# Values of two head pairs made together every second step, with a third pair of turned buffers

## The chip, the cores and the metric

The kernel runs on one core of a Trainium2 chip. The metric is the device time of one execution in microseconds (us). Five engines work side by side, each through its own queue in order: PE multiplies matrices and writes only to the eight banks of PSUM, DVE and ACT compute and copy, POOL does small work and starts some transfers, SP starts transfers. They wait for one another through semaphores. In the profile PE is the row of products and PEld the row of weight loads that go with them.

## The reference

The reference is one step of a small transformer with two layers on 640 tokens (512 latent, 128 context), model width 1024, all in 32-bit floats. In each layer three attentions run side by side, their outputs are joined and projected, and a mixture of 16 experts follows. What is changed here is the latent attention: 8 heads, whose queries and keys have 96 columns and whose values have 64.

```python
k, v = mla_expand(ckv, kpe, w_ukv_l)           # per head: 96 key columns, 64 value columns
s = einsum('bqkgd,bskd->bkgqs', q_blk, k) * scale
p = softmax(s, axis=-1)
o = einsum('bkgqs,bskv->bqkgv', p, v)
x = x + g1 * einsum('bte,ed->btd', heads_out, w_out_l)
```

A latent token reads the 512 latent keys and the 128 context keys, so five blocks of 128; a context token reads the 128 context keys only, one block.

## The kernel before

Each layer runs in stages: modulation and input projection, windowed and neighbourhood attention ("phase 2" in the code), the expansion of queries, keys and values of the latent attention, the latent attention itself ("phase 4"), and the experts. The change touches phase 4, which also holds the output projection, the second norm and the routing.

Phase 4 works on 20 pairs of heads, `pairs[p]`: five tiles of 128 tokens in the order context tile, then four latent tiles, and four pairs of heads for each. Pairs 0 to 3 (context) have one block of keys, `n` = 1; pairs 4 to 19 have `n` = 5. The work is written out by hand in numbered steps `s`, from 0 to 29, the same on every engine. In step `s`, for head `h` = 0 and then 1, PE makes the scores of pair `s` (`scores`, line 588, into banks 0 and 1 or 2 and 3) and turns the normalised probabilities of pair `s-3` (`turn`, transposes, line 520, into banks 4 and 5). Then it makes the values of pair `s-4` (`values`, line 614) into bank 6: one product for each block of keys and head, and the two heads stand in different halves of the 128 columns of the array and of the 128 partitions of the bank. Then comes what the code calls `beside`: for tile `i`, with `PROJ[i]` = 4`i`+8,

- steps `PROJ`+0 and `PROJ`+1: the two halves of the output projection (`out`, line 741, 8 products into bank 7);
- steps `PROJ`+2 and `PROJ`+3: the two halves of the updated tile are transposed (`h2`, line 520, 4 products into bank 7);
- a step with routing logits (line 679) and one with ranks (lines 668 and 669), both into bank 6.

The last tile (`i` = 4) has a table of its own after step 24.

DVE makes in step `s` the row maxima of pair `s` (line 1837), copies the last two turned blocks of pair `s-3` out of bank 5 (line 1871), then evicts what lies in bank 7 in `projected`: line 1926 multiplies a half of the output projection by its gate and line 1927 hands the bank back; line 1930 does this for the second half of `h2`. Only after that it normalises pair `s-1` (lines 1881 and 1884). ACT copies the first three turned blocks (line 1257), takes the exponentials (line 1248), copies the finished values out of bank 6 (`outputs`, line 1262) and evicts the first half of `h2` (line 1305).

The order is held by counters, the lanes: `S` for the score banks, `T` for banks 4 and 5, `O` for bank 6, `M` for bank 7. `take` makes PE wait until everything handed out before on that lane was given back. So each job in bank 7 waits for DVE or ACT to have emptied the job before it. The turned blocks lie in `pt[4]`, two pairs of buffers used in turn; the copy of pair `p` waits for the values of pair `p-2`.

Of the kernel before, what the change touches and what calls it, by code (L numbers as in the profile page):

```python
# [29 lines left out]
ACT = mybir.ActivationFunctionType  # L30
AX = mybir.AxisListType

P = 128
# [39 lines left out]
AT = [ORDER.index(t) for t in range(TILES)]  # L73
# [67 lines left out]
def program(nc, t_in, t_out):  # L141
    with ExitStack() as ctx:
# [18 lines left out]
        hoT = big[:, 1024:6144].rearrange("p (t k n) -> p t k n", t=TILES, k=KD)  # L161
        mrow = sb("mrow", [P, 3, 512])
# [41 lines left out]
        cqT, o = place(0, 2, TOK)  # L204
        ckvT, o = place(o, KEYS)
# [6 lines left out]
        v_loc, o = place(A0, KVT, 384)  # L212
        qs, o = place(o, 2, TOK)
        qn, o = place(o, 2, TOK)
        ksT, o = place(o, KEYS)
        knT, A1 = place(o, 2, KEYS)

        rowG2, o = place(A1, 2, D)
        proj, o = place(o, 2, PW)
        rt, o = place(o, 2, 384)  # L220
        ck, o = place(o, 544)
        junk1, o = place(o, 192)
        assert o <= 4 * 4096
        y1, o = place(4 * 4096, 2, D)
        y2, o = place(o, 2, D)
# [18 lines left out]
        rq, o = place(o, 2, 256)  # L244
        pb4 = ring[:, 0:5120].rearrange("p (a b n) -> p a b n", a=DEEP, b=2)
        pt4a, o = place(A3, 4, 640)
        pt4 = [[pt4a[:, 0], pt4a[:, 1]], [pt4a[:, 2], pt4a[:, 3]]]
        h2T, o = place(o, D)
        junk4, o = place(o, 256)
        r_T, o = place(o, NE)  # L250
# [234 lines left out]
        def value_rows(pr, h, j):  # L485
            if pr["kind"] == "mla":
                return v_mla[:, j, pr["heads"][h] * 64:pr["heads"][h] * 64 + 64]
            at = 64 * h if pr["kind"] == "swa" else 128 + 64 * pr["heads"][h]
            return v_loc[:, j, at:at + 64]

        def column(p, h):
            return slice(2 * (p % 4) + h, 2 * (p % 4) + h + 1)

# [14 lines left out]
        def turned(phase, p, h, w):  # L508

            if phase == 2 and p < WIDE:  # L510
                return ps[:, 4 + h, 0:w]
            return two(2, w) if phase == 2 and p >= APART and h else two(4, w)
# [5 lines left out]
        def _(pe):  # L518
# [52 lines left out]
            def attention(L, phase):  # L571
# [34 lines left out]
                    mm.then_inc(T.full, 1)  # L606

                def values(p):
                    pr = pairs[p]
                    O.take(pe, ("o", L, phase, p))  # L610
                    pe.wait_ge(T.free, T.freed[("p", L, phase, p, 1)])
                    for j in range(pr["n"]):
                        for h in range(2):
                            mm = pe.matmul(ps[64 * h:64 * h + 64, 6, 0:P], value_rows(pr, h, pr["v"][j]),  # L614
                                           pt[phase][p % 2][h][:, j * P:(j + 1) * P],
                                           start=(j == 0), stop=(j == pr["n"] - 1))
                    mm.then_inc(O.full, 1)

                for s in range(STEPS[phase]):
                    turning = 3 <= s < len(pairs) + 3  # L620
                    if phase == 4:
                        ranks(L, s - 1)
                    if phase == 2:
                        together = turning and (s - 3 < WIDE or s - 3 > APART)
                        if turning:
                            turn(s - 3, 0)
                        if together:
                            turn(s - 3, 1)
                        if s < len(pairs):
                            scores(s, (0, 1))  # L630
                        if s in (1, 2):
                            spin(7, 3 - s)
                        if turning and not together:
                            turn(s - 3, 1)
                        if s == len(pairs) + 1:
                            pe.wait_ge(nmax_done, base + 2 * len(pairs))
                        if s > len(pairs):
                            spin(3, 1)
                    else:
                        for h in range(2):  # L640
                            if s < len(pairs):
                                scores(s, (h,))
                                if s == 0:
                                    spin(7, 2)
                            if turning:
                                turn(s - 3, h)
                    if 4 <= s < len(pairs) + 4:
                        values(s - 4)
                    if phase == 2:
                        for g, at in enumerate(MOD_AT):  # L650
                            if s in (at, at + 1) and (g < 2 or L < DEPTH - 1):
                                ks = range(4 * (s - at), 4 * (s - at) + 4)
                                mod_group(L + g // 2, (g + 1) % 3, ks)
                        for g in (1, 2):
                            if s == MOD_AT[g - 1] + 3:
                                mod_columns2(L, g)
                        if s == MOD_AT[2] + 3 and L < DEPTH - 1:
                            mod_columns(L + 1)
                    if phase == 4:
                        if s == 1:  # L660
                            shift_logits(L)
                        beside(L, s)
# [566 lines left out]
        def _(act):  # L1229
            def attention(L, phase):  # L1230
                pairs = PAIRS[phase]
                base = PPL * L + PBASE[phase]

                def exps(p, h):

                    pr, w, col = pairs[p], pairs[p]["n"] * P, column(p, h)
                    buf = pb[phase][:, p % DEEP, h, :]
                    act.wait_ge(nmax_done, base + 2 * p + h + 1)
                    if pr["kind"] == "swa":
                        act.wait_ge(sink_set, SINKS * L + sum(2 * (r["kind"] == "swa") for r in pairs[:p]) + h + 1)  # L1240
                    if phase == 4 and p >= DEEP:
                        act.wait_ge(T.full, T[("p", L, phase, p - DEEP, h)])
                    if phase == 2:
                        w += int(pr["kind"] == "swa")
                        act.activation(buf[:, 0:w], buf[:, 0:w], ACT.Exp, bias=stat["nm"][:, col], scale=-1.0,  # L1245
                                       accum_out=stat["sm"][:, col]).then_inc(ex_done, 1)
                    else:
                        act.activation(buf[:, 0:w], two(2 * h, w), ACT.Exp, bias=stat["nm"][:, col], scale=1.0,  # L1248
                                       accum_out=stat["sm"][:, col]).then_inc(S[h].free, 1)

                def copy(p, h):
                    n = pairs[p]["n"]
                    a, d = split(phase, n)
                    act.wait_ge(T.full, T[("p", L, phase, p, h)])
                    if p >= 2:
                        act.wait_ge(O.full, O[("o", L, phase, p - 2)])
                    act.activation(pt[phase][p % 2][h][:, 0:a * P], turned(phase, p, h, a * P), ACT.Copy).then_inc(T.free, 1)  # L1257

                def outputs(p):
                    pr = pairs[p]  # L1260
                    act.wait_ge(O.full, O[("o", L, phase, p)])
                    act.activation(hoT[:, AT[pr["t"]], pr["chunk"], :], ps[:, 6, 0:P], ACT.Copy).then_inc(O.free, 1)

                for s in range(STEPS[phase]):
                    turning = 3 <= s < len(pairs) + 3
                    if phase == 2:
                        for h in range(2):
                            if turning:
                                copy(s - 3, h)
                        for h in range(2):  # L1270
                            if s < len(pairs):
                                exps(s, h)
                    else:
                        for h in range(2):
                            if turning:
                                copy(s - 3, h)
                            if s < len(pairs):
                                exps(s, h)
                    if 4 <= s < len(pairs) + 4:
                        outputs(s - 4)  # L1280
                    if phase == 4:
                        beside(L, s)
# [406 lines left out]
        def _(dve):  # L1689
# [140 lines left out]
            def attention(L, phase):  # L1830
# [34 lines left out]
                def copy(p, h):  # L1865
                    a, d = split(phase, pairs[p]["n"])
                    if d:
                        dve.wait_ge(T.full, T[("p", L, phase, p, h)])
                        if p >= 2:
                            dve.wait_ge(O.full, O[("o", L, phase, p - 2)])  # L1870
                        dve.tensor_copy(pt[phase][p % 2][h][:, a * P:(a + d) * P], ps[:, 5, 0:d * P]).then_inc(T.free, 1)  # L1871

                def normalise(p):
                    w = pairs[p]["n"] * P
# [533 lines left out]
```

## Time and profile before

| | |
|---|---|
| time, median of 3 runs | 1313.77 us (1312.25 to 1314.42) |
| the profiled execution's own time | 1311.26 us |
| its span, first to last instruction | 1309.3 us |
| PE busy | 1263.0 us, 96% |
| DVE, ACT, POOL busy | 604.7, 354.4, 152.5 us |
| mean granted TensorE clock | 0.992 |
| phase 4 in layer 0 and in layer 1 | about 277 to 441 us and 905 to 1067 us |

PE is busy for 96% of the span, and a product counts as busy until its end, so neighbouring products overlap in the rows: the pace of PE is read from the starts, not from the lengths. A row of the timeline merges instructions of one line that follow each other; its length reaches to the end of the last.

### The profile page before, as it was taken

Reading aid. Unit: us, or ns where it says so; the run is one execution under the profiler, and the core shown is the slowest. Engines: PE = TensorE matmul, PEld = TensorE weight load, DVE = VectorE, ACT = ScalarE, POOL = GpSimd, SP = SyncE. Lnnn points to the kernel's source line nnn. Section 1 sums busy time; section 2 is a strip of 40 time slices with the busy share of each in tenths; the row PEclk is TensorE's granted clock in tenths of the full one; section 3 lists DMA queues with packets and bytes.
Section 4 is the critical chain, followed back from the end, with each engine's and each line's share of the span. In section 5 each row is a group of like instructions: output and inputs, shape, how many; then the busy total and the mean of one; then the engine's idle time right before and its main releaser. Section 6 shows DMA issues by size and latency. Waiting matters only on the chain. (4 is left out here: it accounts for less than half of the span.)

```text
span 1309.3 us, 17044 instructions
## 1 busy us (share of the span) xinstructions
PE 1263.0 (96%) x6010; PEld 724.4 (55%) x6010; DVE 604.7 (46%) x1519; ACT 354.4 (27%) x933; POOL 152.5 (12%) x257
## 2 busy tenths in 40 slices
PE   6999999999999999999999999999999999999997
PEld 3555555565665565444455556566566556444442
DVE  0132266345665553433344235654556646344438
ACT  1121266334433111000012115663433321000001
POOL 2201130000000120000142003000000012000014
PEclk9999999989999999999999999999999999999999
DMA  9977997699011699999694039423001159999966
GB/s 356 364 245 244 316 371 265 227 353 305 25 65 65 242 343 378 366 370 368 242 349 156 17 123 351 151 99 105 1 33 65 65 195 350 391 365 374 367 257 244
DMA packets 125439, 313.13 MB, mean 239 GB/s; under 512 B 9882, under 2 KB 58426, under 8 KB 112688
## 3 DMA queue, kind: packets, MB, share of 16 engines
q1 hardware_dynamic: 90896, 243.13, 51.0%
q0 software_dynamic: 12848, 45.39, 9.1%
q10 hardware_dynamic: 21616, 23.60, 5.4%
q8 instruction: 45, 0.74, 0.2%
q14 instruction: 34, 0.28, 0.1%
HBM read 232.14 MB, written 80.71 MB: 239 GB/s over the span
## 5 line engine op out<-in xcount | busy, mean ns | idle before, releaser
L820 PE MATMUL ps<-ring,big 128*128 128x384 f32 (+2 forms) x640 | 230.6, 519 | 1.5 <-DVE big L1804 1.3
L820 PEld LDWEIGHTS ps<-ring,big 128*128 128x128 f32 x640 | 120.3, 190 | 104.2 <-issue 63.7
L901 PE MATMUL ps<-ring,arena 128*128 128x512 f32 x384 | 169.3, 593 | 1.9 <-ACT arena L1437 1.9
L741 PE MATMUL ps<-ring,big 128*128 128x512 f32 x320 | 143.0, 599 | 0.9
L520 PEld LDWEIGHTS ps<-consts,arena 128*128 128x128 f32 (+2 forms) x880 | 103.6, 143 | 69.1 <-issue 50.9
L588 PE MATMUL ps<-arena 64*128 64x128 f32 (+5 forms) x576 | 136.2, 428 | 2.4 <-ACT ring L1248 1.4
L520 PE MATMUL ps<-consts,arena 128*128 128x128 f32 (+2 forms) x880 | 123.4, 277 | 4.7 <-ACT arena L1390 2.5
L1257 ACT ACTIVATE arena<-ps 128x384 f32<-128x384 f32 (+3 forms) x140 | 67.3, 492 | 199.3 <-PE ps L520 198.5
L901 PEld LDWEIGHTS ps<-ring,arena 128*128 128x128 f32 x384 | 71.2, 190 | 83.1 <-issue 83.1
L588 PEld LDWEIGHTS ps<-arena 64*128 64x128 f32 (+1 forms) x576 | 74.4, 194 | 53.4 <-issue 45.1
L741 PEld LDWEIGHTS ps<-ring,big 128*128 128x128 f32 x320 | 59.0, 190 | 70.5 <-issue 66.4
L1441 ACT ACTIVATE arena<-ps 128x256 f32<-128x256 f32 x32 | 12.3, 385 | 300.6 <-PE ps L901 300.6
L1837 DVE TENSOR_REDUCE st_nm<-ps 128x1 f32<-128x640 f32 (+1 forms) x80 | 57.2, 717 | 74.6 <-PE ps L588 74.2
L614 PE MATMUL ps<-arena 128*64 128x128 f32 x1104 | 85.9, 280 | 1.4 <-DVEq L2005 1.4
L2164 DVE TENSOR_TENSOR arena<-arena,ps 128x256 f32<-128x256 f32 x32 | 13.5, 421 | 154.4 <-ACT arena L1441 154.4
L614 PEld LDWEIGHTS ps<-arena 128*64 128x64 f32 x1104 | 66.5, 137 | 13.1 <-issue 8.4
L2182 DVE TENSOR_TENSOR arena<-ps,arena 128x512 f32<-128x512 f32 x64 | 44.2, 691 | 55.1 <-PE ps L922 55.1
L1248 ACT ACTIVATE ring<-ps,st_nm 128x640 f32<-128x640 f32 (+1 forms) x80 | 56.4, 705 | 19.7 <-DVE st_nm L1837 19.3
L922 PE MATMUL ps<-ring,arena 128*128 128x512 f32 x128 | 57.8, 594 | 1.0 <-DVE arena L2170 1.0
L922 PE MATMUL ps<-arena 128*128 128x512 f32 x128 | 57.8, 594 | 1.0 <-DVE arena L2170 1.0
L1245 ACT ACTIVATE arena<-arena,st_nm 128x640 f32<-128x640 f32 (+4 forms) x80 | 53.6, 673 | 17.3 <-DVE st_nm L1862 16.0
L520 PE MATMUL ps<-consts,ring 128*128 128x128 f32 x336 | 51.9, 278 | 5.3 <-ACT arena L1257 4.4
(238 smaller groups left out, 1467.6 us busy)
## 6 DMA issues: line engine op xcount, KB each, us to landing
ring<-in_w_mod SPq DMA_DIRECT2D x40, 1024.0 KB, 12.1
ring<-in_w_up SPq DMA_DIRECT2D x22, 1024.0 KB, 9.4
ring<-in_w_gate SPq DMA_DIRECT2D x22, 1024.0 KB, 6.8
slots<-zeros ACTq DMA_DIRECT2D x8, 2560.0 KB, 14.7
slots<-zeros SPq DMA_DIRECT2D x8, 2560.0 KB, 20.4
arena<-in_w_down SPq DMA_DIRECT2D x16, 1024.0 KB, 12.3
arena<-slots SPq DMA_DIRECT2D x30, 512.0 KB, 5.5
slots<-arena POOLq DMA_DIRECT2D x30, 512.0 KB, 9.3
```

The costliest lines, as they stand in the source:

```text
L520: return pe.transpose(out, in_, ident)
L588: mm = pe.matmul(two(score_bank(phase, p, h))[:, at:at + hi - lo], queries(pr, h), keys(pr, h, lo, hi), start=(at % 512 == 0), stop=True, ...
L614: mm = pe.matmul(ps[64 * h:64 * h + 64, 6, 0:P], value_rows(pr, h, pr["v"][j]), pt[phase][p % 2][h][:, j * P:(j + 1) * P], start=(j == 0), ...
L741: mm = pe.matmul(ps[:, b, :], hoT[:, i, k, :], slot[2 + half][:, k, :], start=(k == 0), stop=(k == KD - 1))
L820: mm = pe.matmul(ps[:, c, 0:CHUNKS[c][1]], hT[:, s, k, :], slot[c][:, k, 0:CHUNKS[c][1]], start=(k == 0), stop=(k == KD - 1))
L901: mm = pe.matmul(ps[:, b, :], xgT[:, b, k * P:(k + 1) * P], w_gu[q][:, :, k, :], start=(k == 0), stop=(k == KD - 1))
L922: mm = pe.matmul(ps[:, 2 + n, :], hidT[:, b, k * P:(k + 1) * P], w_dn[q][:, k, n * 512:(n + 1) * 512], start=(k == 0), stop=(k == 1))
L1245: act.activation(buf[:, 0:w], buf[:, 0:w], ACT.Exp, bias=stat["nm"][:, col], scale=-1.0, accum_out=stat["sm"][:, col]).then_inc(ex_done, 1)
L1248: act.activation(buf[:, 0:w], two(2 * h, w), ACT.Exp, bias=stat["nm"][:, col], scale=1.0, accum_out=stat["sm"][:, col]).then_inc(S[h].free, 1)
L1257: act.activation(pt[phase][p % 2][h][:, 0:a * P], turned(phase, p, h, a * P), ACT.Copy).then_inc(T.free, 1)
L1837: dve.tensor_reduce(nm, two(2 * h, w), AX.X, ALU.max, negate=True).then_inc(nmax_done, 1)
L2182: return TT(yb[:, b, n * 512:(n + 1) * 512], ps[:, 2 + n, :], rowG[:, n * 512:(n + 1) * 512], ALU.mult)
```

## The change

The values of phase 4 are made in every second step. In odd steps `s` (5 to 23) PE makes the values of pairs `s-5` and `s-4` one behind the other, side by side in bank 6 (columns 0 to 127 and 128 to 255), and ACT copies both out with one instruction of 256 columns. In even steps no values are made and none copied out. Phase 2 stays as it is. Since a pair's turned blocks are now kept one step longer, `pt[4]` has a third pair of buffers, which lies in `mrow`, the rows in which the modulation vectors are made; a wait for `mods_out` (the transfer of these rows to memory, awaited by SP ahead of phase 4 already) stands before its first use.

```diff
-        pt4 = [[pt4a[:, 0], pt4a[:, 1]], [pt4a[:, 2], pt4a[:, 3]]]
+        mflat = mrow.rearrange("p a b -> p (a b)")
+        pt4 = [[pt4a[:, 0], pt4a[:, 1]], [pt4a[:, 2], pt4a[:, 3]], [mflat[:, 0:640], mflat[:, 640:1280]]]
...
+        def turned_rows(phase, p, h):
+            return pt[phase][p % len(pt[phase])][h]
+        def value_group(phase, p):
+            if phase == 2:
+                return (p,)
+            return (p - 1, p) if p % 2 else ()
+        def values_before(phase, p):
+            q = p - len(pt[phase])
+            return q if q < 0 or phase == 2 or q % 2 else q + 1
...
                 def values(p):
-                    pr = pairs[p]
+                    group = value_group(phase, p)
                     O.take(pe, ("o", L, phase, p))
                     pe.wait_ge(T.free, T.freed[("p", L, phase, p, 1)])
-                    for j in range(pr["n"]):
-                        for h in range(2):
-                            mm = pe.matmul(ps[64 * h:64 * h + 64, 6, 0:P], value_rows(pr, h, pr["v"][j]),
-                                           pt[phase][p % 2][h][:, j * P:(j + 1) * P],
+                    for g, q in enumerate(group):
+                        pr = pairs[q]
+                        for j in range(pr["n"]):
+                            for h in range(2):
+                                mm = pe.matmul(ps[64 * h:64 * h + 64, 6, g * P:(g + 1) * P], value_rows(pr, h, pr["v"][j]),
+                                               turned_rows(phase, q, h)[:, j * P:(j + 1) * P],
...
-                    if 4 <= s < len(pairs) + 4:
+                    if 4 <= s < len(pairs) + 4 and value_group(phase, s - 4):
                         values(s - 4)
...
-                    if p >= 2:
-                        act.wait_ge(O.full, O[("o", L, phase, p - 2)])
+                    q = values_before(phase, p)
+                    if q >= 0:
+                        act.wait_ge(O.full, O[("o", L, phase, q)])
+                    if phase == 4 and p == 2:
+                        act.wait_ge(mods_out, 32 * (L + 1))
...
-                    act.activation(hoT[:, AT[pr["t"]], pr["chunk"], :], ps[:, 6, 0:P], ACT.Copy).then_inc(O.free, 1)
+                    n = len(value_group(phase, p))
+                    act.activation(hoT[:, AT[pr["t"]], pr["chunk"] + 1 - n:pr["chunk"] + 1, :],
+                                   ps[:, 6, 0:n * P].rearrange("p (a b) -> p a b", a=n), ACT.Copy).then_inc(O.free, 1)
```

DVE's copy waits in the same way as ACT's, with the wait for `mods_out` at its own first use of the third pair (`p` = 5).

On PE, the end of step 9 and step 10 of layer 0 stand so before (line 588 scores, 520 transposes, 614 values, 741 output projection; `ps` is PSUM, `ring` holds the probabilities and the weights of the projection, `big` the tile that `h2` transposes):

```order
L614 MATMUL ps<-arena 64x128 [waits t_free,o_free]
L614 MATMUL ps<-arena 64x128 x9
L741 MATMUL ps<-ring,big 128x512 [waits o_free,slot3_in,m_free]
L741 MATMUL ps<-ring,big 128x512 x7
...
L588 MATMUL ps<-arena 128x512 [waits s1_free]
L588 MATMUL ps<-arena 128x128
L520 MATMUL ps<-consts,ring 128x128 [waits pn_done,t_free]
L520 MATMUL ps<-consts,ring 128x128 x4
L614 MATMUL ps<-arena 64x128 [waits t_free,o_free]
L614 MATMUL ps<-arena 64x128 x9
L520 MATMUL ps<-consts,big 128x128 [waits res_done,m_free]
L520 MATMUL ps<-consts,big 128x128 x3
```

and so after the change (the lines are those of the changed file: 604 scores, 536 transposes, 632 values, 759 output projection):

```order
L632 MATMUL ps<-arena 64x128 [waits t_free,o_free]
L632 MATMUL ps<-arena 64x128 x9
L632 MATMUL ps<-mrow,arena 64x128 x10
L759 MATMUL ps<-ring,big 128x512 [waits o_free,slot3_in,m_free]
L759 MATMUL ps<-ring,big 128x512 x7
...
L604 MATMUL ps<-arena 128x512 [waits s1_free]
L604 MATMUL ps<-arena 128x128
L536 MATMUL ps<-consts,ring 128x128 [waits pn_done,t_free]
L536 MATMUL ps<-consts,ring 128x128 x4
L536 MATMUL ps<-consts,big 128x128 [waits res_done,m_free]
L536 MATMUL ps<-consts,big 128x128 x3
```

The ten values of step 10 have moved ahead into those of step 11, and the transposes of `h2`, which wait for bank 7 (`m_free`), stand directly behind those of the probabilities.

On ACT, steps 9 and 10 had two copies out of bank 6 (line 1262; 1257 are the copies of turned blocks, 1248 the exponentials):

```order
L1262 ACTIVATE big<-ps 128x128 [waits o_full]
L1257 ACTIVATE arena<-ps 128x384 [waits o_full,t_full]
L1248 ACTIVATE ring,st_sm<-ps,st_nm 128x640 [waits t_full,nmax_done]
L1257 ACTIVATE arena<-ps 128x384 [waits o_full,t_full]
L1248 ACTIVATE ring,st_sm<-ps,st_nm 128x640 [waits t_full,nmax_done]
L1262 ACTIVATE big<-ps 128x128 [waits o_full]
L1292 ACTIVATE arena,ssq<-big 128x512 [waits res_done]
```

and have one of double width at the end of step 9 (the lines of the changed file: 1284, 1278, 1266, 1315):

```order
L1284 ACTIVATE big<-ps 128x256 [waits o_full]
L1278 ACTIVATE arena<-ps 128x384 [waits o_full,t_full]
L1266 ACTIVATE ring,st_sm<-ps,st_nm 128x640 [waits t_full,nmax_done]
L1278 ACTIVATE arena<-ps 128x384 [waits o_full,t_full]
L1266 ACTIVATE ring,st_sm<-ps,st_nm 128x640 [waits t_full,nmax_done]
L1315 ACTIVATE arena,ssq<-big 128x512 [waits res_done]
```

The copy at the end of step 10 is gone; nothing else on ACT has changed its place. DVE's order is the same in both kernels, except that some of its copies go to `mrow`.

## Rows read from the trace of the kernel before

**Rows 1.** The page, busy time of each engine, its share and instructions.
```profile
PE 1263.0 (96%) x6010; PEld 724.4 (55%) x6010; DVE 604.7 (46%) x1519; ACT 354.4 (27%) x933; POOL 152.5 (12%) x257
```
**Rows 2.** Stretches: length, busy time (instructions) of each engine, clock, DMA share, GB/s.
```profile
277.00:441.30 164.30, 158.68 (x924) 101.17 (x922) 91.95 (x230) 62.21 (x173) 8.55 (x15) 0.98 0.41 135
441.30:790.00 348.70, 343.34 (x1120) 183.21 (x1119) 136.01 (x294) 44.40 (x119) 47.36 (x75) 1.00 0.75 279
905.00:1067.00 162.00, 156.99 (x908) 99.17 (x906) 90.90 (x227) 60.84 (x170) 8.53 (x15) 0.97 0.18 61
```
**Rows 3.** PE's timeline, steps 7 to 10: start, length, instructions [idle before].
```profile
304.05 0.44 PE L614 MATMUL ps<-arena 128*64 128x128 f32 x4
304.42 1.35 PE L588 MATMUL ps<-arena 96*128 96x512 f32 x4
305.61 0.71 PE L520 MATMUL ps<-consts,ring 128*128 128x128 f32 x5
306.15 1.25 PE L588 MATMUL ps<-arena 96*128 96x512 f32 x4
307.23 0.71 PE L520 MATMUL ps<-consts,ring 128*128 128x128 f32 x5
307.88 1.31 PE L614 MATMUL ps<-arena 128*64 128x128 f32 x20
309.12 7.13 PE L741 MATMUL ps<-ring,big 128*128 128x512 f32 x16
...
319.44 1.31 PE L614 MATMUL ps<-arena 128*64 128x128 f32 x20
320.87 7.13 PE L741 MATMUL ps<-ring,big 128*128 128x512 f32 x16
...
330.55 0.71 PE L520 MATMUL ps<-consts,ring 128*128 128x128 f32 x5
331.19 1.31 PE L614 MATMUL ps<-arena 128*64 128x128 f32 x20
332.61 0.66 PE L520 MATMUL ps<-consts,big 128*128 128x128 f32 x4
```
**Rows 4.** DVE's timeline, end of step 10.
```profile
331.49 0.41 DVE L1871 COPY arena<-ps 128x256 f32<-128x256 f32 x1
331.82 0.68 DVE L1926 TENSOR_TENSOR big<-ps,arena 128x512 f32<-128x512 f32 x1
```
**Rows 5.** Who waited for whom on PEld: us in total, times, longest.
```profile
PEld ps L588 <- ACT ring L1248: 3.2, 8, 0.9
PEld ps L520 <- DVEq L1927: 2.5, 8, 0.4
PEld ps L741 <- DVEq L1927: 2.5, 8, 0.4
PEld ps L741 <- DVE arena L1930: 1.5, 6, 0.3
```
**Rows 6.** PE's timeline, step 20 and the values of step 23.
```profile
413.57 1.31 PE L614 MATMUL ps<-arena 128*64 128x128 f32 x20
414.82 7.13 PE L741 MATMUL ps<-ring,big 128*128 128x512 f32 x16
...
438.63 1.31 PE L614 MATMUL ps<-arena 128*64 128x128 f32 x20 [0.62 <-DVEq L2005]
```
**Rows 7.** DVE's timeline, end of step 20.
```profile
414.02 0.68 DVE L1930 TENSOR_TENSOR arena<-ps,modc 128x512 f32<-128x512 f32 x1
```
**Rows 8.** Stretches as in rows 2, around low clock and in step 22.
```profile
283.67:287.09 3.42, 2.78 (x25) 2.58 (x24) 0.96 (x5) 0.46 (x3) 0.00 (x0) 1.00 1.04 348
287.09:293.92 6.83, 6.78 (x18) 3.98 (x19) 2.42 (x9) 2.76 (x11) 0.00 (x0) 0.50 1.03 343
911.70:922.00 10.30, 10.17 (x24) 5.23 (x23) 4.01 (x11) 4.62 (x15) 0.00 (x0) 0.50 0.33 123
433.70:438.60 4.90, 3.73 (x39) 3.00 (x37) 2.57 (x9) 2.48 (x8) 0.00 (x0) 1.00 0.04 13
```

More of the change, by code:

```diff
@@ L608, in values @@
                 def values(p):
-                    pr = pairs[p]
+                    group = value_group(phase, p)
                     O.take(pe, ("o", L, phase, p))
                     pe.wait_ge(T.free, T.freed[("p", L, phase, p, 1)])
-                    for j in range(pr["n"]):
-                        for h in range(2):
-                            mm = pe.matmul(ps[64 * h:64 * h + 64, 6, 0:P], value_rows(pr, h, pr["v"][j]),
-                                           pt[phase][p % 2][h][:, j * P:(j + 1) * P],
-                                           start=(j == 0), stop=(j == pr["n"] - 1))
+                    for g, q in enumerate(group):
[4 more added lines that the diff above has]
+                                               turned_rows(phase, q, h)[:, j * P:(j + 1) * P],
+                                               start=(j == 0), stop=(j == pr["n"] - 1))
                     mm.then_inc(O.full, 1)
@@ L1254, in copy @@
                     act.wait_ge(T.full, T[("p", L, phase, p, h)])
-                    if p >= 2:
-                        act.wait_ge(O.full, O[("o", L, phase, p - 2)])
-                    act.activation(pt[phase][p % 2][h][:, 0:a * P], turned(phase, p, h, a * P), ACT.Copy).then_inc(T.free, 1)
+                    q = values_before(phase, p)
[3 more added lines that the diff above has]
+                        act.wait_ge(mods_out, 32 * (L + 1))
+                    act.activation(turned_rows(phase, p, h)[:, 0:a * P], turned(phase, p, h, a * P), ACT.Copy).then_inc(T.free, 1)
                 def outputs(p):
@@ L1278, in attention @@
                                 exps(s, h)
-                    if 4 <= s < len(pairs) + 4:
+                    if 4 <= s < len(pairs) + 4 and value_group(phase, s - 4):
                         outputs(s - 4)
@@ L1868, in copy @@
                         dve.wait_ge(T.full, T[("p", L, phase, p, h)])
-                        if p >= 2:
-                            dve.wait_ge(O.full, O[("o", L, phase, p - 2)])
-                        dve.tensor_copy(pt[phase][p % 2][h][:, a * P:(a + d) * P], ps[:, 5, 0:d * P]).then_inc(T.free, 1)
+                        q = values_before(phase, p)
+                        if q >= 0:
+                            dve.wait_ge(O.full, O[("o", L, phase, q)])
+                        if p == 5:
+                            dve.wait_ge(mods_out, 32 * (L + 1))
+                        dve.tensor_copy(turned_rows(phase, p, h)[:, a * P:(a + d) * P], ps[:, 5, 0:d * P]).then_inc(T.free, 1)
                 def normalise(p):
```

## The prediction, written before the changed kernel ran

> **What bounds the kernel now.** I read the page first, then the stretches, then the timelines around the values. PE is busy for 1263.0 us of 1309.3 [rows 1]. In phase 4 it is busy for 158.68 of 164.30 us in layer 0 and 156.99 of 162.00 in layer 1, and in the experts of layer 0 for 343.34 of 348.70 [rows 2]; DVE and ACT have much time left everywhere. So PE's own sequence sets the time: what is added to it or taken from it reaches the end of the kernel almost whole, because the experts behind it have no wait that could swallow it. The question is how long PE takes from the start of step 4 to the end of step 23.
>
> **What a group of values costs.** PE's pace is read from starts [rows 3]. Five transposes followed by scores take 306.15 - 305.61 = 0.54 us; followed by values they take 307.88 - 307.23 = 0.65, so entering the group costs 0.11. The twenty rows of one pair (each 32-bit product is two) take until 309.12, so 1.24. Without the group the projection could start at 307.23 + 0.54 = 307.77; the group costs 309.12 - 307.77 = 1.35 there. Behind it the first product is slow as well: four scores take 1.35 us behind values and 1.25 behind transposes, 0.10 more. One group standing alone costs 1.45 us. The pace inside: four rows last 0.44, twenty 1.31, so 0.87/16 = 0.054 each, and twenty more rows appended to a group cost 20 x 0.054 = 1.09. A merge that is bare of waits therefore saves 1.45 - 1.09 = 0.36 us. There are 10 merges per layer, 20 in all: up to 7.2 us. That is the whole possible gain on PE.
>
> The Trainium skill, "TensorEngine Tiling (Array Packing)", section "Key Properties", gives a reason for such a saving: a change of the tiling mode drains the engine. The rows agree that both edges of the group cost something (0.11 and 0.10 us); by that rule alone the change would bring the 7.2 us, to about 1306.6.
>
> **What the group hides.** Behind the values of most steps stands a job for bank 7, and it waits until DVE has emptied that bank. DVE reaches this eviction only after its copy of the last turned blocks, that is, after the transposes directly ahead of the values. Step 10 shows it: the transposes start at 330.55 and end 0.71 later at 331.26 [rows 3]; DVE copies from 331.49, multiplies out of bank 7 from 331.82 to 332.50 [rows 4]; PE goes on at 332.61 [rows 3]. PE could have gone on at 330.55 + 0.54 = 331.09. All 1.52 us between are DVE's chain, and the values lie inside it. Take them away and PE starts the next job at 332.61 all the same: this step saves nothing. The waits that stick out behind the values today mark the places [rows 5]: 8 times the transposes of `h2` behind line 1927 (steps 10, 14, 18, 22 of two layers), 6 times the projection behind line 1930 (steps 12, 16, 20), and 8 times the projection behind line 1927 (odd steps 9, 13, 17, 21).
>
> **The sum, over two layers.**
> - Odd steps 9 to 23, eight per layer: each gets ten more products behind those it has, 16 x 1.09 = +17.4 us. In step 23 the values wait for the ranks first (0.62, line 2005 [rows 6]); this wait is ahead of the group and hides nothing of the addition.
> - Step 8: nothing is in bank 7 to wait for, since the projection of tile 0 is the first job there since step 1, and in the rows it starts without an idle time [rows 3]. Its group goes whole: 2 x -1.45 = -2.9.
> - Even steps 10, 12, 14, 16, 18, 22: 0 each, hidden in DVE's chain. If the cover were only partly needed, each would save up to 1.45 (12 x 1.45 = 17.4 at the other end). I take 0, because rows 3 and 4 show the chain to run past the group already and its start, the end of the transposes, does not move.
> - Step 20: DVE is done at 414.02 + 0.68 = 414.70 [rows 7], PE went on at 414.82 [rows 6]: at most 0.1 each, I take 2 x -0.05 = -0.1.
> - Odd steps 9, 13, 17 had a wait left behind the values: 320.87 - 319.44 = 1.43 instead of 1.24 [rows 3], 0.19. A double group covers it: 6 x -0.18 = -1.1. Step 21 shows none.
> - Steps 4 to 7, pairs with one block (four rows, 0.44 long [rows 3]): the scores there wait for exponentials anyway (3.2 us in 8 waits [rows 5]), so a removed group of four rows saves little, and four rows more in steps 5 and 7 cost 4 x 0.054 = 0.2 each, partly in those waits. I take +0.1 per layer, +0.2. The ends: four small groups removed whole, each up to about 0.5, would be -2.0; nothing hidden, +0.9.
> - ACT's copy of 256 columns in place of two of 128, and the new wait for `mods_out`: 0. ACT is busy for 62 of 164 us of the phase [rows 2], its one copy per two steps stands ahead of nothing that PE awaits before the next turned blocks, and the transfer had ended before phase 4 began (SP waited for it). Were the wait real, ACT's copies and exponentials from step 5 on would queue behind it.
> - The wait of the turned-block copies for earlier values: always values of a step before; those precede the transposes on PE. 0.
>
> Sum: 17.4 - 2.9 - 0.1 - 1.1 + 0.2 = +13.5 us. Against the profiled execution's own 1311.26 this is 1324.8; that execution lies 2.5 under the median of the runs shown, so for the median 1313.77 + 13.5 = 1327.3.
>
> **Rival 1: the clock falls as well.** The granted clock was at its lower level (1.2 instead of 2.4 GHz) from 287.09 to 293.92 and for about 10.3 us from 911.7 [rows 8]; ahead of the first, PE was busy for only 2.78 of 3.42 us, much of it with products of 24 columns. At the end of phase 4 there are already stretches in which PE does little but transposes, rank products and waits: 433.7 to 438.6 has 3.73 us busy in 4.90 [rows 8], and 1.2 of these are the values of step 22, which now go. Step 20 is of the same kind (a wait for ACT between its transposes, then, without values, one of 1.1 us). So up to two places per layer could bring the lower level. Each such stretch, 6.8 to 10.3 us long, costs half its length, 3.4 to 5.1 us, since dense projection products follow. With one or two of them in the whole kernel 1331 to 1337, with four up to 1347. Against it: the stretches did not drop the clock before, and the gaps of 1.5 us in steps 10 to 18 stand between dense work. The Trainium skill, "TensorE: Matmul & The Clock Gate", Part 4 on the PE-mode transpose, says that transposes do not count as busy in the way that products do; that would speak for this rival, and no row here shows it by itself.
>
> **Rival 2: the gain comes through (the other side).** If DVE emptied bank 7 earlier than its place in the order suggests, the even steps would be bare and all 20 merges would save 0.36: -7.2, 1306.6. It decides at the chain's length: DVE would have to be done within 0.54 us of the start of the transposes, not 1.95 (330.55 to 332.50) as in rows 3 and 4. Nothing in the change moves DVE's instructions, so this speaks against it.
>
> **Rival 3: half of it.** Some even steps save part of their group, because later starts give DVE time to catch up elsewhere, or because a wait in the odd steps (turned blocks in steps 11 and 15) shrinks. At half of the added cost in the even steps, 6 x 0.6 x 2 = 7 us less: 1320. At equal chance of no net effect, 1313.8, it would take 1.1 us from each of the twelve even steps, which none of the chain's rows supports.
>
> **How the numbers follow.** Forecast (stalls, clock as before) 0.52; clock falls too 0.32; half of it 0.08; no net effect 0.04; the gain 0.04. The forecast's own range is 1324 to 1330, from the ends of steps 4 to 7 and run-to-run noise. The range of 8 in 10 takes in most of rival 1 and the upper part of rival 3: 1319 to 1338. What a measurement of this kernel can tell is about 0.2% or 2.6 us. Faster 0.04, same 0.04, slower 0.92.
>
> **What would show it.** The values group appears as 40 rows, about 2.4 us long, eight times per layer, with no idle before the job behind it in odd steps. In the even steps 10 to 22 PE's row has a new idle time of 1.2 to 1.6 us ahead of `h2` or the projection, put down to DVE, about 14 in two layers and some 19 us in total; PE's busy time stays nearly the same while the span grows. In step 8 the projection starts 0.54 us after the transposes. A third and fourth low stretch in the clock near the end of phase 4 would be rival 1. The prediction is wrong if the idle times in the even steps are well under 1 us, or if the odd steps' additional products take less than 1.09 us.

## The result, and the profile after

The changed kernel takes 1329.24 us (median of 4 runs, 1325.61 to 1332.50) against 1314.10 for the kernel before (1312.25 to 1315.38): a ratio of 1.0116, with its 95% interval 1.0093 to 1.0138. Its profiled execution took 1327.09 us, its span is 1325.1. The comparison of the totals comes first. The second row is the busy time of each engine in the page of the changed kernel:

```profile
span 1325.1 us, 17004 instructions
PE 1261.8 (95%) x6010; PEld 726.3 (55%) x6010; DVE 604.9 (46%) x1519; ACT 351.7 (27%) x913; POOL 152.4 (12%) x257
```

Against [rows 1] PE has as many instructions and is busy for 1.2 us less, with a span 15.8 us longer. The loss is idle time on PE, and the waits name it. PE's waits in the trace of the changed kernel (us in total, times, longest):

```profile
PE ps L536 <- DVEq L1953: 10.5, 8, 1.4
PE ps L759 <- DVE arena L1956: 7.4, 6, 1.3
PE ps L604 <- ACT ring L1266: 3.4, 6, 0.7
PE ps L536 <- ACT arena L1278: 2.3, 4, 0.6
PE ps L536 <- ACT mrow L1278: 1.2, 2, 0.6
```

Two rows of the same view of the kernel before, for ACT's copies of turned blocks and for the exponentials:

```profile
PE ps L520 <- ACT arena L1257: 4.4, 6, 1.1
PE ps L588 <- ACT ring L1248: 1.4, 2, 0.7
```

The first two rows of the changed kernel are new: 14 waits, 17.9 us in all, for DVE's products out of bank 7. The numbers of lines have moved: 536 is 520 of before (transposes), 604 is 588 (scores), 632 is 614 (values), 759 is 741 (projection), 1953 and 1956 are 1927 and 1930, 1897 is 1871 (DVE's copy of turned blocks), 1860 is 1837 (maxima). The first 8 and the next 6 are exactly the even steps 10 to 22 of both layers. PEld's rows, which answer to [rows 5], say the same; the 8 waits of the projection for line 1927, in the odd steps, have gone:

```profile
PEld ps L536 <- DVEq L1953: 12.4, 8, 1.6
PEld ps L759 <- DVE arena L1956: 8.8, 6, 1.5
PEld ps L604 <- ACT ring L1266: 5.1, 8, 0.9
```

PE's timeline of the changed kernel, the end of steps 8, 9 and 10 (start, length, instructions, [idle before]), answers to [rows 3]:

```profile
308.98 0.71 PE L536 MATMUL ps<-consts,ring 128*128 128x128 f32 x5
309.53 0.59 PE L759 MATMUL ps<-ring,big 128*128 128x512 f32 x1
...
319.11 0.71 PE L536 MATMUL ps<-consts,ring 128*128 128x128 f32 x5
319.75 1.31 PE L632 MATMUL ps<-arena 128*64 128x128 f32 x20
320.89 1.26 PE L632 MATMUL ps<-mrow,arena 128*64 128x128 f32 x20
322.08 0.70 PE L759 MATMUL ps<-ring,big 128*128 128x512 f32 x1
...
331.76 0.71 PE L536 MATMUL ps<-consts,ring 128*128 128x128 f32 x5
333.83 0.55 PE L536 MATMUL ps<-consts,big 128*128 128x128 f32 x3 [1.35 <-DVEq L1953]
```

In step 8 the projection follows the transposes at once. In step 9 both pairs run together: 322.08 - 319.75 = 2.33 us, against 1.43 before. In step 10 PE stands still for 1.35 us. From the start of the transposes to the next job it takes 333.83 - 331.76 = 2.07 us; before, with the values in between, it took 332.61 - 330.55 = 2.06 [rows 3]. So the step costs the same with its values and without. DVE at that place in the changed kernel:

```profile
331.96 0.82 DVE L1860 TENSOR_REDUCE st_nm<-ps 128x1 f32<-128x640 f32 x1 [0.48 <-PE ps L604]
332.70 0.41 DVE L1897 COPY arena<-ps 128x256 f32<-128x256 f32 x1
333.03 0.68 DVE L1952 TENSOR_TENSOR big<-ps,arena 128x512 f32<-128x512 f32 x1
```

It is the chain of [rows 4]: maxima, copy of the turned blocks, product out of bank 7 until 333.71, and PE goes on 0.12 us later.

Two stretches show the whole phase, from the start of step 8 to the first product of `out(4,0)`; first the kernel before, then the changed one (length, busy time and instructions of each engine, clock, DMA share, GB/s):

```profile
304.42:441.32 136.90, 132.88 (x797) 83.56 (x795) 77.73 (x193) 48.62 (x130) 8.57 (x15) 1.00 0.28 94
```

```profile
306.17:450.81 144.64, 132.89 (x796) 84.67 (x795) 77.64 (x192) 47.21 (x122) 9.65 (x16) 0.99 0.27 90
...
370.40:373.70 3.30, 1.95 (x13) 1.35 (x12) 3.05 (x7) 2.81 (x9) 0.00 (x0) 1.00 0.02 5
373.70:377.10 3.40, 3.40 (x10) 2.17 (x9) 2.00 (x9) 1.48 (x4) 1.24 (x2) 0.50 0.69 217
1052.90:1056.30 3.40, 3.40 (x6) 1.33 (x4) 1.68 (x3) 0.00 (x0) 0.00 (x0) 0.50 0.00 0
```

PE is busy for the same 132.9 us and the stretch is 7.74 us longer. 1.7 of these are not idle time: from 373.70 to 377.10 the clock stands at its lower level (1.2 GHz; the column says 0.50 of 2.4). Just ahead of it PE was busy for 1.95 us of 3.30, with the new idle time of step 14 in between. Layer 1 has a stretch like it from 1052.90, behind step 20. At neither place had the trace of the kernel before a low stretch. A part of every comparison here is time lost at the lower clock, and it differs from run to run of one kernel. So beside each median stands a second number. The time lost at the low clock is estimated as (1 - mean granted clock) x span of the same run, as if PE set the pace all through the low stretches; the time less this loss is called the corrected time below. The clock of a run is on record to three digits, so one run's corrected time is known to about 0.7 us. For 29 runs of the kernel before beside the first four experiments it is 1299.5 us at the median (1297.4 to 1301.6), where the times themselves go from 1309.8 to 1321.1; for the four runs of the changed kernel it is 1313.1 (1311.4 to 1313.8). These two sets did not run side by side; a second pair that did gives 1300.5 and 1313.8 (after_again, below). The change costs 13.6 us in corrected time, and the time lost at the low clock grew from 14.4 to 16.6 us at the medians.

### The profile page after: what moved, and what is told of

The parts are those of the page before. It is cut to its first block and busy times, and to the rows that moved or that the text cites. A ratio compares the mean times of both kernels' runs of the same rounds, so it can differ in the third digit from the quotient of the medians.

```text
span 1325.1 us, 17004 instructions
## 1 busy us (share of the span) xinstructions
PE 1261.8 (95%) x6010; PEld 726.3 (55%) x6010; DVE 604.9 (46%) x1519; ACT 351.7 (27%) x913; POOL 152.4 (12%) x257
## 5 line engine op out<-in xcount | busy, mean ns | idle before, releaser
L604 PE MATMUL ps<-arena 64*128 64x128 f32 (+5 forms) x576 | 135.6, 427 | 4.3 <-ACT ring L1266 3.4
L604 PEld LDWEIGHTS ps<-arena 64*128 64x128 f32 (+1 forms) x576 | 74.6, 195 | 54.4 <-issue 44.5
L1278 ACT ACTIVATE arena<-ps 128x384 f32<-128x384 f32 (+3 forms) x116 | 56.4, 499 | 158.2 <-PE ps L536 158.0
L2190 DVE TENSOR_TENSOR arena<-arena,ps 128x256 f32<-128x256 f32 x32 | 13.5, 421 | 154.4 <-ACT arena L1464 154.4
L632 PE MATMUL ps<-arena 128*64 128x128 f32 x896 | 69.6, 278 | 1.4 <-DVEq L2031 1.4
L1266 ACT ACTIVATE ring<-ps,st_nm 128x640 f32<-128x640 f32 (+1 forms) x80 | 56.4, 705 | 19.3 <-DVE st_nm L1860 19.0
L632 PEld LDWEIGHTS ps<-arena 128*64 128x64 f32 x896 | 55.7, 136 | 8.4 <-issue 3.7
## 6 DMA issues: line engine op xcount, KB each, us to landing
ring<-in_w_mod SPq DMA_DIRECT2D x40, 1024.0 KB, 11.9
arena<-in_w_down SPq DMA_DIRECT2D x16, 1024.0 KB, 11.8
```

Of the source, the lines that this page charges most:

```text
L604: mm = pe.matmul(two(score_bank(phase, p, h))[:, at:at + hi - lo], queries(pr, h), keys(pr, h, lo, hi), start=(at % 512 == 0), stop=True, ...
L632: mm = pe.matmul(ps[64 * h:64 * h + 64, 6, g * P:(g + 1) * P], value_rows(pr, h, pr["v"][j]), turned_rows(phase, q, h)[:, j * P:(j + 1) * ...
L1278: act.activation(turned_rows(phase, p, h)[:, 0:a * P], turned(phase, p, h, a * P), ACT.Copy).then_inc(T.free, 1)
```

## The experiments

Theory: DVE's place for the eviction of bank 7 makes the even steps as long without their values as with them. Rivals: the removed values would have been free anyway; the new buffers and their waits cost something; the clock costs it.

**DVE empties bank 7 first, in the changed kernel (after_evict_first).** The call of `projected` goes ahead of the maxima and the copies, except for the first projection:

```diff
+                        if s - 1 != PROJ[0]:
+                            projected(L, s - 1)
...
-                    if phase == 4 and s >= 1:
+                    if phase == 4 and s - 1 == PROJ[0]:
```

> The changed kernel with one thing moved: in each step of phase 4 (but the one of the first projection half) DVE empties bank 7 at the start of its step, ahead of its row maxima and copies, and not behind the copy of the last turned blocks. Theory (the loss is DVE's chain behind the transposes, which the values covered): the 14 idle times of 1.1 to 1.5 us in the even steps vanish, about 18 to 20 us; all merges then pay 0.36 us each. Against before: minus 7 for the merges, minus 1 to 2.5 for the waits that before has behind its values, so 1304 to 1308 us where before has 1314. Rival (the clock's additional low stretches are a main part of the loss): the time stays 3 to 5 us above that. Rival (DVE's own work is too long for an early place, since it then delays the maxima by 0.7 us in every step): part of the idle time comes back ahead of scores or transposes, 1310 to 1320 us.

Measured: 1310.21 us (12 runs, 1308.07 to 1312.86), a ratio of 0.9971 (0.9955 to 0.9987) to the kernel before; corrected 1297.2, so 15.9 less than the change. PE's timeline, steps 10 and 11, and the waits of this kernel:

```profile
332.19 0.71 PE L536 MATMUL ps<-consts,ring 128*128 128x128 f32 x5
332.74 0.60 PE L536 MATMUL ps<-consts,big 128*128 128x128 f32 x4
333.18 1.25 PE L604 MATMUL ps<-arena 96*128 96x512 f32 x4
334.26 0.71 PE L536 MATMUL ps<-consts,ring 128*128 128x128 f32 x5
334.81 1.25 PE L604 MATMUL ps<-arena 96*128 96x512 f32 x4
337.12 0.76 PE L536 MATMUL ps<-consts,ring 128*128 128x128 f32 x5 [1.06 <-DVE mrow L1897]
337.81 2.40 PE L632 MATMUL ps<-arena 128*64 128x128 f32 x40
```

```profile
PE ps L536 <- DVE arena L1897: 6.9, 8, 1.2
PE ps L536 <- DVE mrow L1897: 2.1, 2, 1.1
```

All 14 waits for bank 7 are gone: behind the transposes of step 10 the next job starts after 0.55 us. That shows where the idle time came from: DVE's order, and not the work of the even steps. The intervals of the 14 steps shrink by 20.2 us (from 1.63, 1.57, 1.39 and 1.45 to 0.11 between the starts of the last transpose and of the next job), yet only 15.9 arrive, and the time is above the 1304 to 1308 us that were expected. Ten waits for DVE's copies of turned blocks, 9.0 us, stand where the changed kernel has two such waits, 0.8 us, and 2.3 us more for ACT's copies. That is 5.9 us more of waits for copies, enough for the missing 4.3, though these waits were not taken away by themselves. In step 11 the copy stands behind maxima which could start only when an earlier product of DVE was done, and PE's transposes wait for the copy. This is DVE's timeline there:

```profile
335.31 0.69 DVE L2054 TENSOR_TENSOR big<-big,arena 128x512 f32<-128x512 f32 x1
335.92 0.82 DVE L1860 TENSOR_REDUCE st_nm<-ps 128x1 f32<-128x640 f32 x1
336.65 0.41 DVE L1897 COPY mrow<-ps 128x256 f32<-128x256 f32 x1
```

**The same order without merged values (before_evict_first).** The same edit in the kernel before.

> The kernel before, with the same move of DVE's eviction of bank 7 to the start of the step and nothing else. Theory: the 22 short waits behind the values go, which stick out by 0.1 to 0.2 us each: minus 1 to 3 us, 1311 to 1313 us, so that the change's two parts interact: merging costs 15 us with the late eviction and gains 5 to 7 with the early one. Rival (the early eviction is a gain by itself of 10 us or more, whatever the values do): 1304 us or less.

Measured: 1314.35 us (12 runs), ratio 1.0006 (0.9989 to 1.0023), where 1311 to 1313 was expected; corrected 1297.1, so 2.4 less than before and level with after_evict_first. The 2.4 us do not show in the time, since 17.1 us are lost at the low clock, against 14.4 in the kernel before: the trace of this kernel has low stretches in phase 4 at 427.4 and 1052.0, where the kernel before has none, and one of 17 us from 287.5, where it has 6.8. In times the merged kernel is 4.1 us ahead, and 4.0 of that is the difference in time lost at the low clock (17.1 against 13.1). In the 12 runs of each the loss is 13.1 to 21.1 us here and 11.8 to 14.4 in after_evict_first, so this is more than scatter; whether the merged values bring it or something else was not tried. The order alone is worth 2.4 us corrected where the values stand in every step, and 15.9 (1313.1 - 1297.2) where they are merged: only there had PE been left with nothing else to do. That merging brings nothing in corrected time under this order was not expected. Here PE waits less for the copies than in after_evict_first:

```profile
PE ps L520 <- DVE arena L1871: 4.6, 4, 1.2
```

That is 4.4 us less than the 9.0 there, and the waits for exponentials are 1.4 us against 2.7. Together 5.7 of the 7.2 us that merging could have saved stand in these waits; that they ate the saving is read from the two traces and was not tested.

**The third buffers without the merging (third_buffers_alone).**

```diff
-            if phase == 2:
-                return (p,)
-            return (p - 1, p) if p % 2 else ()
+            return (p,)
...
-            return q if q < 0 or phase == 2 or q % 2 else q + 1
+            return q
```

> The changed kernel with its values made in every step again, one pair each, and copied out singly; only the third pair of turned buffers in the modulation rows and the waits for them are left of the change. Theory: as before, 1313 to 1315 us, since the copies never waited for the values of an earlier step. Rival (the rows in mrow or their wait for mods_out cost something): over 1317 us, with idle time of ACT ahead of the copy of pair 2.

Measured: 1314.55 us (10 runs), ratio 1.0009 (0.9988 to 1.0030); corrected 1299.1 against 1299.5. The buffers in the modulation rows and the wait for `mods_out` cost nothing that can be measured. One wait is shorter in this trace than before: between the transposes of step 20 PE waits 0.58 us for ACT's copy in each layer, where it waited 1.05 and 1.01. In sum its waits for ACT's copies are 3.5 us in 6 waits, against the 4.4 in 6 above.

**Products on zeros in the idle times (after_spin, and again beside a second run of the change, after_again).** Ahead of bank 7's job of the even steps 10 to 22 PE gets two products on zeros (four rows) into bank 6, once ACT has emptied it, to see whether the clock hangs on the idle time:

```diff
+                    if phase == 4 and s in (10, 12, 14, 16, 18, 20, 22):
+                        pe.wait_ge(O.free, O.frees)
+                        spin(6, 2)
```

> The changed kernel with two filler products of 256 columns of zeros into bank 6 (0.85 us on PE) in steps 10, 12, 14, 16, 18, 20 and 22, where PE otherwise stands idle for 1.1 to 1.5 us. Theory: the fillers lie inside the idle time, which stays put down to DVE, so they cost nothing; and PE is active in it, so the additional low stretches of the clock in phase 4 (one in each layer of the profiled run) go: 1325 to 1328 us and less scatter than the 7 us of the changed kernel. Rival (the low stretches have nothing to do with the idle times): the same low stretches and 1325 to 1333 us. Rival (the eviction is not what PE waits for): the fillers add to the time, up to 12 us.

Measured: 1324.34 us (6 runs, 1323.58 to 1327.64); corrected 1313.2, the same as the change's 1313.1. Repeated together:

> The changed kernel itself, beside the run with fillers on the same chip. Theory: 1326 to 1333 us; with the low clock taken off 1312.5 to 1313.5 us, that is 13 to 14 above before's 1299.5, as forecast; the rest of its loss is time at the low clock, which differs from run to run.

> The changed kernel with the fillers in the even steps, as in after_spin, on the same chip as after_again. Theory (the idle times of the even steps bring some of the low stretches): 2 to 5 us below after_again, and as much in the time at the low clock; with that taken off, equal within 0.5 us. Rival (the difference between the first two sets was chance of the runs): the two within 1 us, also in the time at the low clock.

Measured: after_again 1328.99 us (4 runs, 1326.14 to 1331.44), corrected 1313.8; after_spin_again 1327.36 (5 runs, 1325.35 to 1328.08), corrected 1315.0. Step 10 in the trace of after_spin, and the stretches around the place where the clock of the changed kernel had dropped:

```profile
331.64 0.71 PE L536 MATMUL ps<-consts,ring 128*128 128x128 f32 x5
332.19 1.03 PE L541 MATMUL ps<-zeros 128*128 128x256 f32 x4
333.71 0.66 PE L536 MATMUL ps<-consts,big 128*128 128x128 f32 x4 [0.49 <-DVEq L1956]
```

```profile
370.00:373.40 3.40, 2.91 (x19) 2.22 (x18) 3.11 (x7) 2.85 (x10) 0.00 (x0) 1.00 0.00 0
373.40:380.00 6.60, 6.60 (x64) 4.98 (x63) 4.35 (x14) 4.02 (x11) 2.23 (x3) 1.00 0.76 277
```

The step is as long as in the changed kernel (333.71 - 331.64 = 2.07 us): the added 1.03 us lie wholly inside the idle time. The clock stays at 2.4 GHz there, and neither filled trace has a low stretch in phase 4 from step 8 on; after_again has two, in layer 1 (1045.1 to 1048.5 and 1055.3 to 1058.7), and a third right behind the phase (from 1082.6). The time lost at the low clock falls by 5.4 us in the first pair (16.6 to 11.2) and 4.0 in the second (15.9 to 11.9); in the 8 runs without the products on zeros it is 10.6 to 20.0, in the 11 with them 9.3 to 13.3. The times differ by 4.9 and by 1.6 us; the second is below what was expected, since the corrected time of those runs was 1.2 us higher, about the scatter of this number over a few runs. So products in the idle times take away some of the low clock, worth 2 to 5 us in the two pairs, but not the 13.6 us. They take away more than the change had brought: 11.2 and 11.9 us are less than the 14.4 and 13.1 of the kernel before.

**Merged values with an order made for them (merged_order), and that order alone (single_order).** From the experiments so far: values of the first four pairs single again, DVE empties bank 7 early, in steps 21 and 22 between the copies of the two heads, and in steps 11, 15 and 19 the copy goes ahead of the maxima.

```diff
-            if phase == 2:
+            if phase == 2 or p < 4:
                 return (p,)
...
+                    late, between = s - 1 == PROJ[0], s in (21, 22)
...
+                        if not late and not between:
+                            projected(L, s - 1)
...
+                        copy_first = phase == 4 and h == 0 and s in (11, 15, 19)
+                        if copy_first:
+                            copy(s - 3, h)
...
+                        if phase == 4 and h == 0 and between:
+                            projected(L, s - 1)
```

> The changed kernel (values of two pairs together) with DVE's order in phase 4 fitted to it: bank 7 emptied at the start of the step, in steps 21 and 22 between the copies for the two heads; in steps 11, 15 and 19 the copy of the turned blocks of head 0 ahead of the row maximum, not behind it; and the values of the four short pairs made singly again in steps 4 to 7. Theory: with bank 7 emptied early the merges' 7 us went into new waits of PE for DVE's copies of turned blocks (0.67 us more in each of steps 11, 15 and 19, 0.65 in steps 21 and 22, in both layers); with these copies early, 5 to 8 us come back: 1302 to 1306 us where the kernel before has 1314 and the same kernel with the early eviction alone 1310. With the time lost at the low clock taken off ((1 - mean granted clock) x span), 1289 to 1292 after 1297. Rival (DVE's backlog only moves on to the maxima and so to the scores): 1308 to 1311 us, waits of scores for exponentials in steps 12, 16 and 20.

> The kernel before (values of one pair in each step) with the same order of DVE as the run beside it (bank 7 emptied early, copy of head 0 first in steps 11, 15, 19). Theory: merging is worth 0.36 us for each of 16 merges of full pairs once nothing waits, so this one lies 4 to 6 us above merged_order; it gains 1 to 2 us on the early eviction alone from the copies (waits of 0.57, 0.07 and 0.07 us per layer) and up to 1 us from step 22: 1294 to 1296 us with the low clock taken off. Rival (merging is worth nothing in itself, the edges of the group are hidden in some other limit): the two within 1.5 us of each other.

Measured: merged_order 1306.88 us (6 runs, 1305.28 to 1310.33), ratio 0.9951 (0.9936 to 0.9965), corrected 1293.4; single_order 1311.28 (10 runs, 1306.74 to 1317.31), ratio 0.9985 (0.9967 to 1.0002), corrected 1295.8; the kernel before beside them 1313.41, corrected 1300.5. merged_order stays above what was expected of it (1302 to 1306 us, corrected 1289 to 1292), and single_order lies where it was expected in corrected time. merged_order beats both kernels: it is 0.49% faster than before, against 1.16% slower for the change. Merging in this order is worth 4.4 us in times and 2.4 corrected, more than the rival of no gain allowed (1.5 us). The bare saving of 8 merges per layer, 16 x 0.36 = 5.8 us, does not come whole. Steps 10 and 11 of merged_order:

```profile
334.78 0.71 PE L536 MATMUL ps<-consts,ring 128*128 128x128 f32 x5
335.33 0.60 PE L536 MATMUL ps<-consts,big 128*128 128x128 f32 x4
335.76 1.25 PE L604 MATMUL ps<-arena 96*128 96x512 f32 x4
336.85 0.71 PE L536 MATMUL ps<-consts,ring 128*128 128x128 f32 x5
337.39 1.25 PE L604 MATMUL ps<-arena 96*128 96x512 f32 x4
339.02 0.77 PE L536 MATMUL ps<-consts,ring 128*128 128x128 f32 x5 [0.38 <-ACT mrow L1278]
339.71 2.40 PE L632 MATMUL ps<-arena 128*64 128x128 f32 x40
```

```profile
PE ps L536 <- ACT mrow L1278: 2.3, 4, 0.8
PE ps L604 <- ACT ring L1266: 1.4, 2, 0.7
PE ps L759 <- DVE arena L1964: 1.4, 2, 0.7
```

The chain behind bank 7 is gone in these steps, and the copy's wait in step 11 is down from 1.06 to 0.38 us, now for ACT. With the first four pairs single the waits for exponentials are back at the 2 of 1.4 us of the kernel before. (In layer 0 of that trace the clock was low over most of these steps, from 287.4 to 304.5; in layer 1 it was low only until 919, ahead of steps 5 and 7, and no wait stands there either.) The waits of single_order for the same things are these:

```profile
PE ps L520 <- ACT arena L1257: 3.8, 6, 0.8
PE ps L588 <- ACT ring L1248: 1.2, 4, 0.4
```

That is 5.0 us. merged_order has 7.4: the three rows above and 2.3 us for ACT's other copies. So 2.4 of the 3.4 us between the bare saving and the measured one stand in waits that single_order does not have, the largest of them the two ahead of the projection, 1.4 us for bank 7. None was taken away by itself, and the last 1.0 us stays open.

## Why the prediction was right

The forecast was 1327.3 us, the measured median is 1329.24, inside both ranges. Its sum was +13.5 us, with the clock as before. In times the change costs 15.1 us (1329.24 - 1314.10); in corrected time 13.6, and 13.3 in the repeated runs (1313.8 - 1300.5). That it comes this close is in part luck, since two terms that the sum missed or had too small cancel (step 20 and steps 4 to 7 below). The likeliest case was the right one by its mechanism too. By its terms:

- **Odd steps, +17.4.** Confirmed. From the start of the last transpose to the job behind the values it was 1.44 us where nothing was waited for, 1.63 in steps 9, 13 and 17; afterwards it is 2.54 in every step from 9 to 21. That is 1.10 in the bare case, where 1.09 was taken. At the seam of the two pairs nothing is lost (320.89 - 319.75 = 1.14 for the first twenty rows).
- **Their waits, -1.1.** Confirmed: 1.63 became 2.54, +0.91, so 0.19 given back in each of the six steps.
- **Step 8, -2.9.** Confirmed: 309.53 - 308.98 = 0.55 us in place of 309.12 - 307.23 = 1.89 [rows 3], with the 0.10 of the slow first product 1.44 in place of 1.45.
- **Even steps 10 to 18 and 22, 0.** Confirmed to 0.01 us: the same interval was 1.63, 1.57, 1.63, 1.57, 1.63, 1.44 before and 1.63, 1.57, 1.63, 1.57, 1.63, 1.45 after. 14 new idle times were forecast, of 1.2 to 1.6 us and some 19 us in sum; there are 14, the longest 1.4, 17.9 in sum. after_evict_first shows the cause: moving DVE's instruction removes all 14 of them and 15.9 us.
- **Step 20, -0.1.** Confirmed: 1.44 became 1.39. Beside it, in the same step, something was missed: the wait for ACT between its transposes (1.05 us before) is 0.63 now, 0.4 us per layer that the sum didn't have. Merging is not needed for it: third_buffers_alone has 0.58 at this place. Nor are the new buffers alone the reason, since before_evict_first, with the old ones, has 0.58 in both layers too. What sets it stays open.
- **Steps 4 to 7, +0.2.** Too small. From the first scores of step 4 to step 8 layer 0 took 290.29 to 306.17 = 15.88 us; before 288.86 to 304.42 = 15.56. That is +0.32 per layer, +0.6 in all if layer 1 is alike. The prediction said that the scores there wait for exponentials anyway, and read this from PEld's rows. PE itself had no such wait in these steps: its 2 waits of 1.4 us in sum stand in step 3. Now they are 6 of 3.4 (L604 on L1266 above); the new four stand in steps 5 and 7, 0.46 to 0.53 each, behind steps without values, and they are gone in merged_order. Here too removed groups came back as idle time, for another engine. In after_again only two of the four are there. This point and the one before it cancel.
- **Buffers, `mods_out` and the copy of double width, 0.** No cost: third_buffers_alone takes 1314.55 us against 1313.88. In its trace step 20 is shorter by 0.9 us in the two layers, too little to tell in the time (corrected 1299.1 against 1299.5). The copy of double width was not tried by itself.
- **The whole.** 2 x (3 x 0.91 + 5 x 1.10) - 2.9 - 0.1 + 0.6 - 0.8 = +13.3 us by the measured terms.
- **Rival 1, the clock.** Held in part, beside the forecast and smaller. It foresaw places where PE thins out; there are two new stretches in phase 4, 3.4 us each and not 6.8 to 10.3, so 1.7 us each. One of them is where it was looked for (behind step 20 in layer 1), the other where it was argued against (step 14 of layer 0, one of the gaps "between dense work"). At the medians of the runs it comes to 2 us. The runs with products on zeros show that idle time has a part in it.
- **Rival 2, the gain.** Refuted for the change as made. Its condition, DVE done within the time of the transposes, holds in after_evict_first (1310.21) and in merged_order, which took 1306.88 against the 1306.6 that the rival named; but that is luck and no match of the sums, since the order alone brought 4.7 us corrected there (1300.5 - 1295.8) and the merging 2.4, not the 5.8 of its 16 merges. Rival 3 and no net effect: refuted by the equal intervals above.

The row that carried all this was the pair [rows 3] and [rows 4]: PE's next start lay 0.11 us behind DVE's end, not behind its own values.

## What to carry to other kernels

A job on the bound engine is only worth removing if the job behind it could start earlier: look for what else must have ended by then, and compare that end, not the engine's busy share. Here 12 of the 20 removed groups (and two more nearly) lay inside another engine's chain and cost nothing, so moving them into steps that hide nothing cost 0.91 to 1.10 us each. Order the engine that hands back the bank first, then merge: together, with the first four pairs left single, that is 0.49% faster than before, the merge alone 1.16% slower, and the order alone 0.15% faster, within the noise.

## What was not expected of the hardware

- Nearly all the scatter of one kernel is time at the lower clock. In 29 runs of the kernel before the time goes over 11.3 us (1309.8 to 1321.1), the time lost at the low clock over 11.9 (10.5 to 22.4), and the difference of the two over 4.2. Two kernels a few us apart are told apart better by the corrected time, as long as both numbers are shown: a kernel can bring low clock of its own, as before_evict_first seems to, and the corrected time hides that.
- A low stretch of 3.4 us in layer 0 followed 3.3 us in which PE was busy for 1.95; the longest of all traces here, in third_buffers_alone, lasted 20.5 us from 908.1. With 1.03 us of products on zeros in the idle times, neither trace has a low stretch from step 8 on.
- Two pairs of values back to back have no seam, though the second reads other buffers: twenty rows take 1.14 us up to the next pair (320.89 - 319.75), against 1.24 up to a job on 128x128 weights (309.12 - 307.88 [rows 3]).
